# Attention on one core: the logits two items ahead, and the turn of the softmax weights, change places in TensorE's order

## The reference

```python
score = einsum('bths,bth->bts', relu(qi . k_idx * IDX_DIM**-0.5), wi)   # where admissible, else -inf
_, sel = lax.top_k(score, n_sel)
logits = einsum('btkgd,btnkd->btkgn', qg, k[sel]) * HEAD_DIM**-0.5
p = softmax(where(valid, logits, -inf))
o = einsum('btkgn,btnkd->btkgd', p, v[sel])
x = x + concat(conv_out, attn_out) @ w_out
```

## Time and profile before

| | |
|---|---|
| median of three runs | 1181.89 us (1181.59 to 1183.21) |
| profiled execution | 1183.32 us |
| its span, first to last instruction | 1181.5 us |
| TensorE busy | 1164.3 us (99%) |
| VectorE busy | 921.2 us (78%) |
| ScalarE busy | 521.4 us (44%) |
| mean granted clock of TensorE | 0.997 |

### The profile page before, as it was taken

The page is one execution under the profiler, slowest core; times in us unless marked ns, Lnnn a source line. Parts: engine busy times, 40 slices in busy tenths (PEclk is TensorE's granted clock), DMA queues, the critical chain, the costliest instruction groups (busy, mean ns, idle before and its releaser), DMA issues.

```text
span 1181.5 us, 20455 instructions
## 1 busy us (share of the span) xinstructions
PE 1164.3 (99%) x7800; PEld 1119.3 (95%) x7800; DVE 921.2 (78%) x1405; ACT 521.4 (44%) x788; POOL 62.5 (5%) x73
## 2 busy tenths in 40 slices
PE   8999999999999999999999999999999999999999
PEld 8999999999999999857999688999999999999998
DVE  5799777776989982368998754778977878798995
ACT  5354444544545552351223552534544444454452
POOL 0000000000000000003573000000000000000000
PEclk9999999999999999999999999999999999999999
DMA  7202222221342233211321021331221222234221
GB/s 257 72 37 108 71 88 90 71 107 53 111 149 98 72 106 119 72 36 37 143 72 37 1 66 59 138 107 37 75 105 71 103 74 73 79 106 152 101 98 69
DMA packets 21920, 103.98 MB, mean 88 GB/s; under 512 B 3296, under 2 KB 4960, under 8 KB 12384
## 3 DMA queue, kind: packets, MB, share of 16 engines
q1 hardware_dynamic: 20976, 99.28, 23.9%
q10 hardware_dynamic: 880, 3.82, 1.0%
HBM read 96.99 MB, written 6.10 MB: 87 GB/s over the span
## 4 chain that ended last, share of the span: by engine, by line
PE 85%; DVE 9%; issue 3%; ACT 2%; DMA 1%; ACTq 0%; DVEq 0%
PE ps L601 16%; PE ps L602 16%; PE ps L603 16%; PE ps L548 8%; PE ps L552 8%; PE ps L550 8%; PE ps L539 2%; PE ps L541 2%; PE ps L540 2%; PE ps L799 1%; PE ps L922 1%; PE ps L882 1%; PE ps L808 1%; ACT wh L1042 1%; DVE wl L1587 1%
## 5 line engine op out<-in xcount | busy, mean ns | idle before, releaser
L1042 ACT ACTIVATE wh<-raw 128x1024 fp32r<-128x1024 f32 (+3 forms) x201 | 201.6, 1004 | 267.3 <-PE ps L603 146.2
L601 PE MATMUL ps<-xs,wh 128*128 128x320 f32 x976 | 301.7, 309 | 1.8 <-DVE wl L1587 1.8
L602 PE MATMUL ps<-xs,wh 128*128 128x320 f32 x976 | 301.5, 309 | 0.0
L603 PE MATMUL ps<-xs,wl 128*128 128x320 f32 x976 | 301.5, 309 | 0.0
L601 PEld LDWEIGHTS ps<-xs,wh 128*128 128x128 f32 x976 | 183.3, 188 | 2.4 <-DVE wl L1587 2.3
L602 PEld LDWEIGHTS ps<-xs,wh 128*128 128x128 f32 x976 | 183.3, 188 | 0.0
L603 PEld LDWEIGHTS ps<-xs,wl 128*128 128x128 f32 x976 | 183.2, 188 | 0.0
L548 PE MATMUL ps<-xh,wh 128*128 128x320 f32 x568 | 135.7, 320 | 0.0
L552 PE MATMUL ps<-xh,wl 128*128 128x320 f32 x568 | 130.3, 311 | 0.0
L550 PE MATMUL ps<-xl,wh 128*128 128x320 f32 x568 | 130.0, 310 | 0.0
L1587 DVE TENSOR_TENSOR wl<-raw,wh 128x1024 fp32r<-128x1024 f32 (+1 forms) x108 | 112.6, 1043 | 18.9 <-ACT wh L1042 17.7
(11 more groups left out here) (265 smaller groups left out, 2102.2 us busy)
## 6 DMA issues: line engine op xcount, KB each, us to landing
raw<-gu SPq DMA_DIRECT2D x43, 1024.0 KB, 4.8
raw<-dn SPq DMA_DIRECT2D x16, 1024.0 KB, 4.9
raw<-dn SPq DMA_DIRECT2D x12, 512.0 KB, 3.8
raw<-wconv SPq DMA_DIRECT2D x6, 1024.0 KB, 4.8
raw<-wout SPq DMA_DIRECT2D x4, 1024.0 KB, 4.8
raw<-wtok SPq DMA_DIRECT2D x4, 840.0 KB, 4.3
x<-xt SPq DMA_DIRECT2D x8, 320.0 KB, 4.8
x_keep<-x SPq DMA_DIRECT2D x8, 320.0 KB, 2.2
```

The costliest lines, as they stand in the source:

```text
L601: pe.matmul(out, ah, bh, start=first, stop=False, skip_group_check=True)
L602: pe.matmul(out, ah, bl, start=False, stop=False, skip_group_check=True)
L603: return pe.matmul(out, al, bh, start=False, stop=last, skip_group_check=True)
L1042: return nc.scalar.activation(out, in_, ACT.Copy, scale=scale)
```

## The change

Two lines change places: in item n the logits of item n + 2 now stand ahead of the turn of item n.

```diff
--- before.py
+++ after.py
@@ -1017,9 +1017,9 @@
                     proj_part(12 + (i - 32) // 4, i % 4)
 
             for n in range(len(ITEMS)):
-                turn_weights(n)
                 if n + 2 < len(ITEMS):
                     logits(n + 2)
+                turn_weights(n)
                 for i in range(parts_by(n - 1), parts_by(n)):
                     filler(i)
                 if n > 8 and n % 8 == 1 and ITEMS[n - 2][0] != 4:
```

## The result

| | before | changed |
|---|---|---|
| median, 7 runs each | 1181.85 us (1181.58 to 1183.24) | 1185.86 us (1184.25 to 1187.38) |
| ratio, 95% interval | | 1.0032 [1.0021, 1.0043] |
| timed again with other kernels, later | 1183.03 us | 1185.76 us, 1.0028 [1.0018, 1.0037] |
| profiled execution, span | 1183.32, 1181.5 | 1187.25, 1185.5 |
| mean granted clock in it | 0.997 | 0.995 |

The change makes the kernel slower by 0.3%.

What follows compares the result with a forecast made beforehand. TensorE, busy for 99% of the span, was taken to bound the kernel. Terms 0.43 + 0.65 + 0.74 + 1.25 + 0.25 = +3.3 on the profiled 1183.32 gave 1186.6; forecast 1186.2 us, range 1182.2 to 1187.9.

Steps and rivals of the forecast that it cites:

- The lost cover: Items 12, 20, 36, without filler: logits no longer cover ScalarE's copy before the weighing; +0.74, +0.65, +0.43 us.
- Items 8 to 10: Bank 4 some 0.95 us later, item 10's turn out of the stall's shadow (+0.30); together +1.25 us.
- the chain that was named: Frees bank 4: copy of item 9's weights, exponent of item 11, attention output's high part, then low part on VectorE.
- Items 26 and 34: Same stall as item 10; only the weights' turns come out of its shadow, +0.25 us for both (0 to 0.6).
- Item 28: Would pay some 0.6 us, but costed at nothing: the wait of 0.96 at item 32 covers it.
- The gaps: 13 items with logits and filler: gaps of 0.17 us where logits begin and end; taken as 0, bounds 2.2 either way.
- The clock: Low-clock stretch at 657 to 661 us, 1.7 us lost, paid by some executions; the longer stall puts it in the median.
- rival 1: Path cost of +3.3 is right, but the median execution keeps its clock: 1185.2 us; chance 0.22.
- rival 2: One gap per item vanishes and ScalarE's chain takes up item 8's delay: +0.2, 1182.1 or 1183.5 us; chance 0.20.
- rival 3: The stall at item 10 goes instead of growing: 1180.0 us from the median, 1179.7 from the profile; chance 0.08.
- rival 4: A second low-clock stretch at items 32 to 36: 1187.9 us; chance 0.04.

Runs made afterwards that it cites:

- experiment 2: Against the kernel before: logits ahead of the turn at all items but 8, 12, 20, 28 and 36; 1181.57 us, ratio 0.9998.
- experiment 6: The changed kernel with a filler at items 12, 20, 28 and 36 too; 1182.94 us.
- experiment 10: Against the kernel before: logits ahead of the turn at items 12, 20, 28 and 36 only; 1183.84 us, ratio 1.0015.
- experiment 1: Against the kernel before: logits ahead of the turn only at items 8, 12, 20, 28 and 36; 1182.72 us, ratio 1.0010.
- experiment 9: Against the kernel before: logits ahead of the turn at items 8 and 9 only; 1183.39 us, ratio 1.0002.
- experiment 3: Against the kernel before: logits ahead of the turn except at items 8, 9, 10, 12, 20, 26, 28, 34, 36; 1180.96 us, ratio 0.9993.
- experiment 4: Against the kernel before: same order, but filler ahead of the waiting logits at items 10, 26 and 34; 1179.16 us, ratio 0.9972.
- experiment 5: Against the kernel before: same order, with a filler at items 12, 20, 28 and 36 too; 1182.39 us.

## Why the prediction was right, and where not

**The lost cover: right.** From weighing to weighing, item 12 takes 0.75 more (2.11 to 2.86; forecast 0.74), item 20 0.82 more (1.94 to 2.76; 0.65), item 36 0.57 more (0.81 to 1.38; 0.43). The last two cost more than forecast mainly because, behind a weighing of a prompt tile, the logits start later than the turn did (0.78 against 0.61 at item 20, 0.26 against 0.17 at item 36). Experiments 2, 6 and 10 show the cause: without these items, or with a filler in them, the cost is gone.

**Items 8 to 10: right in size.** Bank 4 came 0.92 later (0.95), by the chain that was named, and from the weighing of item 7 to that of item 11 it is 1.10 more (the forecast was 1.25). The stall is longer than 1.84, as the prediction asked, but not by the delay of bank 4: the turn left it. Experiments 1, 2 and 9 add what the sum did not see: with item 8 alone turned round the delay is 0.26, with item 9 alone 0.07, with both 0.92. Only together do they use up ScalarE's slack.

**Items 26 and 34: right,** 0.22 by the timelines (0.25).

**Item 28: right that it costs nothing, wrong about how.** It lost 0.68, and from the weighing of item 27 to that of item 32 the kernels differ by 0.06. But the wait at item 32 did not shrink by it (0.96 to 0.89). It came back earlier: items 29 to 31 are 0.75 shorter together, and the waits for ScalarE's copy at items 29 and 31 (0.25 and 0.23) are gone.

**The gaps: mis-sized.** The sum took 0 from bounds of -2.2 and +2.2 (13 items; there are 14 with logits and a filler); experiment 3 shows -0.73. Of the two gaps per item only one moved: the turn's weight load still starts 0.17 late behind logits (650.80 in the changed kernel), as the nearest row had it, but behind a weighing of tile 4 the logits start as soon as the turn did. This makes nearly all of the difference between the forecast sum of 3.3 and the measured 2.55. The terms above as measured come to 3.46; with 0.73 off for the gaps and 0.06 for item 28 that is 2.7. The Trainium skill (TensorE: Matmul & The Clock Gate, section "Step-by-step: what each phase is for") says that TensorE pulls weight loads ahead under a running matmul. Behind the logits the trace differs from it, by the 0.17 at 650.80; the third of 2.2 that was saved comes from the other gap.

**The clock: the step that failed.** The prediction read the spread of the three times as executions with and without the stretch behind item 10, and let the change bring that stretch into the median. All 76 executions of before in the experiments' timings show some lower clock, and the profile places it behind item 10; experiments 1 and 4, which shorten the stall, lift it. The spread is the other stretch, at 20 to 40 us, which is there with and without the change; the prediction took the trace to have one stretch, and it has two. The forecast of 1186.2 met 1185.86 by luck: the median of those seven runs carries the early stretch and that of before does not, which the prediction did not foresee. Against before's group at 0.997, where the profiled execution stood, the change costs 2.6 and not 2.9. Of the rivals, 1 is right that the change brings no new stretch behind item 10, but its 3.3 was too much by the gaps, and the median did not keep its clock; 2 and 3 fell with bank 4, which came back 0.92 later; the second stretch of rival 4, at items 32 to 36, was not seen. The lower end of the range should have been rival 2's 1182.1, not 1182.2, and it left rival 3 outside.

## What to carry to other kernels

Before a step is moved ahead, ask what it covers where it stands: here matmuls that needed nothing lay between a transpose and the matmuls that read its copy from another engine, and moved ahead they left a wait of 0.4 to 0.7 us at each place that had no other work. Work that is ready belongs into the stall: the same fillers behind or ahead of a waiting step, at three places, made 2.5 us, and 1.5 more where the lower clock behind the stall went with it. And where the clock has two levels, compare executions of equal mean clock before a difference of medians is put down to a change, and look in the profile where the lower level stood: equal means can come from different stretches.

## What was not expected of the hardware

Behind a stall of TensorE of 1.84 to 2.38 us the granted clock fell to the lower level for a stretch (a mean of 0.91 over the 20 us from 650 to 670), at a cost of some 1.5 us; behind one of 1.41 or 1.15 it did not in the profiled executions. With 1.84 or 1.85 none of 108 executions (before, experiments 3, 5 and 10) was without lower clock, and with 2.38 none of 39. The length of the stall alone does not decide, though: with 1.90, in experiment 9, and a wait of 0.67 that ends some 4 us ahead of it, two of ten executions had no lower clock at all. The stretch at 20 to 40 us came in none, one or two pieces from one execution to the next of the same kernel; what brings it was not tried.
